# Hybrid encoder step, one core: two buffers of combined inputs, a later subtraction, and other places for the first norm's sums

## What is computed

```python
h = x + 0.5 * swiglu(rmsnorm(x, g_ffn1), w1g, w1u, w1d)       # FFN 1, width 2816
u = rmsnorm(h, g_mix)
h = h + attention(u @ w_in, caches) @ w_out                    # two head groups
h = h + 0.5 * swiglu(rmsnorm(h, g_ffn2), w2g, w2u, w2d)       # FFN 2, the same shape
y = rmsnorm(h, final_norm)
# swiglu(x, wg, wu, wd) = (silu(x @ wg) * (x @ wu)) @ wd
# rmsnorm(x, g)         = x * rsqrt(mean(x * x) + eps) * g
```

## Time and profile before

| | |
|---|---|
| median of 3 runs | 1183.85 us |
| the profiled execution | 1185.94 us |
| its span | 1184.2 us |
| PE busy | 1090.8 us, 92% of the span |
| DVE busy | 709.8 us, 60% |
| ACT busy | 483.7 us, 41% |
| POOL busy | 103.3 us, 9% |
| TensorE clock granted, mean | 0.953 |

### The profile page before, as it was taken

The page is one execution under the profiler, slowest core; times in us unless marked ns, Lnnn a source line. Parts: engine busy times, 40 slices in busy tenths (PEclk is TensorE's granted clock), DMA queues, the critical chain, the costliest instruction groups (busy, mean ns, idle before and its releaser), DMA issues.

```text
span 1184.2 us, 18922 instructions
## 1 busy us (share of the span) xinstructions
PE 1090.8 (92%) x7786; PEld 1054.2 (89%) x7786; DVE 709.8 (60%) x1051; ACT 483.7 (41%) x817; POOL 103.3 (9%) x93
## 2 busy tenths in 40 slices
PE   6969999999999999878998859996999999999995
PEld 5969999999999999766787639996999999999994
DVE  4887852388874333645687644487784248887234
ACT  5435541155553333233334543333663125565221
POOL 5000000000000110412132101200000000000012
PEclk7989999999999999888999869998999999999997
DMA  5222222232223233300111102222223223322202
GB/s 187 71 74 105 78 81 93 89 107 77 102 74 99 70 101 118 118 21 1 46 50 58 50 1 72 89 91 88 72 86 92 91 72 108 107 72 78 95 25 80
DMA packets 22372, 94.42 MB, mean 80 GB/s; under 512 B 2896, under 2 KB 5968, under 8 KB 17552
## 3 DMA queue, kind: packets, MB, share of 16 engines
q1 hardware_dynamic: 22288, 93.23, 23.3%
HBM read 88.24 MB, written 4.98 MB: 79 GB/s over the span
## 4 chain that ended last, share of the span: by engine, by line
PE 75%; DVE 15%; ACT 5%; issue 4%; POOL 2%; DVEq 0%; POOLq 0%; ACTq 0%
PE acc L661 35%; PE acc L592 33%; PE acc L754 3%; DVE w_lo L1284 1%; POOL ssq L1752 1%; ACT c_hi L1025 1%; DVE comb L1389 1%; ACT w_hi L948 1%; PE acc L849 1%; DVE st L1581 1%; DVE st L1574 1%; ACT probs L1167 1%; ACT probs L1177 1%; DVE rrow L1412 1%; DVE probs L1615 1%
## 5 line engine op out<-in xcount | busy, mean ns | idle before, releaser
L1284 DVE TENSOR_TENSOR w_lo<-raw,w_hi 128x1024 fp32r<-128x1024 f32 (+3 forms) x145 | 175.7, 1212 | 269.2 <-ACT w_hi L948 268.9
L661 PE MATMUL acc<-c_hi,w_hi 128*128 128x288 f32 x1008 | 300.3, 298 | 21.3 <-DVE w_lo L1284 21.3
L661 PE MATMUL acc<-c_lo,w_hi 128*128 128x288 f32 x1008 | 301.0, 299 | 0.0
L661 PE MATMUL acc<-c_hi,w_lo 128*128 128x288 f32 x1008 | 300.8, 298 | 0.0
L948 ACT ACTIVATE w_hi<-raw 128x1024 fp32r<-128x1024 f32 (+3 forms) x145 | 148.3, 1023 | 186.6 <-PE acc L592 171.9
L592 PE MATMUL acc<-h_hi,w_hi 128*128 128x288 f32 x960 | 210.7, 300 | 7.8 <-DVE w_lo L1284 7.4
L661 PEld LDWEIGHTS acc<-c_hi,w_hi 128*128 128x128 f32 x1008 | 191.6, 190 | 21.8 <-DVE w_lo L1284 21.8
L592 PE MATMUL acc<-h_lo,w_hi 128*128 128x288 f32 x960 | 209.2, 298 | 0.0
L592 PE MATMUL acc<-h_hi,w_lo 128*128 128x288 f32 x960 | 208.8, 297 | 0.0
L661 PEld LDWEIGHTS acc<-c_lo,w_hi 128*128 128x128 f32 x1008 | 191.5, 190 | 0.0
L661 PEld LDWEIGHTS acc<-c_hi,w_lo 128*128 128x128 f32 x1008 | 191.0, 190 | 0.0
(11 more groups left out here) (198 smaller groups left out, 1369.1 us busy)
## 6 DMA issues: line engine op xcount, KB each, us to landing
raw<-in_w1gu SPq DMA_DIRECT2D x18, 1024.0 KB, 4.8
raw<-in_w2gu SPq DMA_DIRECT2D x18, 1024.0 KB, 4.8
raw<-in_w1d SPq DMA_DIRECT2D x16, 704.0 KB, 4.1
raw<-in_w2d SPq DMA_DIRECT2D x16, 704.0 KB, 4.0
raw<-in_w_qk SPq DMA_DIRECT2D x13, 512.0 KB, 3.8
raw<-in_w1gu SPq DMA_DIRECT2D x8, 512.0 KB, 4.4
raw<-in_w_out SPq DMA_DIRECT2D x8, 512.0 KB, 3.5
raw<-in_w2gu SPq DMA_DIRECT2D x8, 512.0 KB, 3.7
```

The lines of the kernel that those rows point to most:

```text
L661: m = nc.tensor.matmul(acc[:, banks[side(f)], 0:HALF], w_part[:, col:col + P], x_part[:, k, c, :], start=n in (P1, P5, P2) and k == 0 and ...
L1284: return nc.vector.tensor_tensor(cols, src, hi.bitcast(FP32), ALU.subtract).then_inc(split_ready, 1)
```

## The change

- `comb` becomes two buffers, used in turn by columns; `combine` of column j waits for `combine_lo` of column j - 2. The buffers of the snapshots of the seven products (`snap_g`, `snap_u`) are laid over the second one, `w_sum` over the first.
- On DVE `hidden_lo` of a column moves to the next column, ahead of its `gate_out`, and `combine_lo` of a column moves to the next column, behind its `combine`. The last plain column makes both its own `combine_lo` and the one before.
- In FFN 1, column 0, the up block of column 1 is split earlier: ACT's part directly behind `rms`, DVE's directly behind the reciprocal.
- The squares of the first norm are added on DVE, the first sum inside the loop of the inputs' low parts at d = 4, the other six behind that loop. POOL no longer does this, and its loop over the other norms is written out.
- `norm_sums` moves to k-step 6: of the up block in FFN 1, of the gate block in FFN 2.
- The warm-up is 44 matmuls instead of 12.
- `side`, `X_AT` and the slots of `h_hi` and `h_lo` are written in another way with the same values for PLAIN = 4; `if f < KH` is always true here. `o_b` changes its place in memory with `mix_lo`.

```diff
-WARM_UP = 12
+WARM_UP = 44
...
-            comb = sb("comb", [P, 2 * KH, HALF], FP32, ffn_mem)
+            comb = sb("comb", [P, 2, 2 * KH, HALF], FP32, ffn_mem)
...
-            snap_g = sb("snap_g", [P, 2, 2, HALF], FP32, ffn_mem)
-            snap_u = sb("snap_u", [P, 2, HALF], FP32, ffn_mem)
+        snaps = comb[:, 1]
+        snap_g = snaps[:, 0:4, :].rearrange("p (b t) n -> p b t n", b=2)
+        snap_u = snaps[:, 4:6, :]
...
# gate_up_block (TensorE)
-                    if f == 0 and part == 1 and k == 2:
+                    if f == 0 and part == 1 - ffn and k == KD - 2:
                         norm_sums(2 * ffn, NORM_BANK)
...
# plain_gate_up (ACT)
                 if f == 0:
                     rms(NORMS_BEFORE[ffn_no], NORM_BANK)
+                    if ffn_no == 0:
+                        hi_block(("gu", ffn_no, 1, 1))
                 silu(ffn_no, f)
...
-                comb_hi(ffn_no, f)
+                if f < KH:
+                    comb_hi(ffn_no, f)
                 if f + 1 < PLAIN:
-                    hi_block(("gu", ffn_no, f + 1, 1))
+                    if ffn_no or f:
+                        hi_block(("gu", ffn_no, f + 1, 1))
                     hidden_hi(ffn_no, f)
...
# the inputs' low parts (DVE)
                 u_lo_part(0, d)
                 if d == 0 or d == KD - 1:
                     lo_block(("gu", 0, 0, min(d, 1)))
+                if d == KH:
+                    dve.wait_ge(sq_ready, 2)
+                    nc.vector.tensor_tensor(ssq[:], sq[:], up[:], ALU.add).then_inc(ssq_added, 2)
+            for d in range(2, KD):
+
+                dve.wait_ge(sq_ready, d + 1)
+                dve.wait_ge(ssq_added, d)
+                nc.vector.tensor_tensor(ssq[:], ssq[:], (sq, up)[d % 2][:], ALU.add).then_inc(ssq_added, 1)
...
# combine (DVE)
-                if ffn_no or j:
-
-                    dve.wait_ge(c_ready, KH * ffn_no + j)
+                b = comb[:, j % 2]
+                if j > 1 or ffn_no:
+
+                    dve.wait_ge(c_ready, KH * ffn_no + max(j - 1, 0))
...
# plain_gate_up (DVE)
                 if f == 0:
                     dve.wait_ge(rms_done, NORMS_BEFORE[ffn_no] + 1)
                     nc.vector.reciprocal(rrow[:], rrow[:]).then_inc(r_ready, 1)
+                    if ffn_no == 0:
+                        lo_block(("gu", ffn_no, 1, 1))
                     dve.wait_ge(r_ready, NORMS_BEFORE[ffn_no] + 1)
-                gate_out(ffn_no, f)
-                combine(ffn_no, f)
+                else:
+                    hidden_lo(ffn_no, f - 1)
                 if f + 1 < PLAIN:
+                    gate_out(ffn_no, f)
+                    if f < KH:
+                        combine(ffn_no, f)
+                    if f:
+                        combine_lo(ffn_no, f - 1)
                     up_out(ffn_no, f)
-                    lo_block(("gu", ffn_no, f + 1, 1))
+                    if ffn_no or f:
+                        lo_block(("gu", ffn_no, f + 1, 1))
                     hidden(ffn_no, f)
-                    combine_lo(ffn_no, f)
-                    hidden_lo(ffn_no, f)
                 else:
+                    gate_out(ffn_no, f)
+                    combine(ffn_no, f)
+                    combine_lo(ffn_no, f - 1)
                     combine_lo(ffn_no, f)
                     weight_sums(ffn_no, PLAIN)
...
# sums (POOL)
-                with gp.Fori(0, KD - 1 if norm == 3 else KD) as d:
+                for d in range(KD - 1 if norm == 3 else KD):
...
-            clear_sums(0)
-            with gp.Fori(0, KD // 2) as i:
-                for j in range(2):
-
-                    gp.wait_ge(sq_ready, 2 * i + j + 1)
-                    gp.wait_ge(ssq_added, 2 * i + j)
-                    nc.gpsimd.tensor_tensor(ssq[:], ssq[:], (sq, up)[j][:], ALU.add).then_inc(ssq_added, 1)
             sums(1)
```

More of the change, by code:

```diff
@@ L48 @@
 PARTS = 7
+X_AT = PLAIN - 1
+H_SLOTS = max(CHUNK_F, X_AT + KD)
 EPS = 1e-6
@@ L271, in hybrid_step @@
             c_lo = sb("c_lo", [P, KH, PARTS, HALF], FP32R, ffn_mem)
-            h_hi = sb("h_hi", [P, CHUNK_F, TOK], FP32R, ffn_mem)
-            h_lo = sb("h_lo", [P, CHUNK_F, TOK], FP32R, ffn_mem)
-            comb = sb("comb", [P, 2 * KH, HALF], FP32, ffn_mem)
+            h_hi = sb("h_hi", [P, H_SLOTS, TOK], FP32R, ffn_mem)
+            h_lo = sb("h_lo", [P, H_SLOTS, TOK], FP32R, ffn_mem)
+            comb = sb("comb", [P, 2, 2 * KH, HALF], FP32, ffn_mem)
             gate = sb("gate", [P, TOK], FP32, ffn_mem)
             up = sb("up", [P, TOK], FP32, ffn_mem)
-            snap_g = sb("snap_g", [P, 2, 2, HALF], FP32, ffn_mem)
-            snap_u = sb("snap_u", [P, 2, HALF], FP32, ffn_mem)
-        w_sum = comb[:].rearrange("p c n -> p (c n)")[:, 0:4 * PART].rearrange("p (s n) -> p s n", s=4)
-        X_AT = CHUNK_F - KD
+        snaps = comb[:, 1]
+        snap_g = snaps[:, 0:4, :].rearrange("p (b t) n -> p b t n", b=2)
+        snap_u = snaps[:, 4:6, :]
+        w_sum = comb[:, 0].rearrange("p c n -> p (c n)")[:, 0:4 * PART].rearrange("p (s n) -> p s n", s=4)
         with ExitStack() as att_mem:
@@ L297, in hybrid_step @@
             ident = am("ident", [P, P])
+            o_b = am("o_b", [P, 2, TOK_TILES, P])
             mix_lo = am("mix_lo", [P, KD, TOK], FP32R)
-            o_b = am("o_b", [P, 2, TOK_TILES, P])
             sq_o = am("sq_o", [P, TOK_TILES, P])
@@ L407, in side @@
         def side(f):
-            return (f - PLAIN if f < CHUNK_F else f - CHUNK_F) % 2
+            return (f if f < CHUNK_F else f - CHUNK_F) % 2
         def pairs_before(ffn, f):
@@ L1023, in comb_hi @@
                 act.wait_ge(comb_ready, KH * ffn_no + j + 1)
-                nc.scalar.activation(c_hi[:, j, 0, :], comb[:, 0, :], ACT.Copy)
-                nc.scalar.activation(c_hi[:, j, 1:PARTS, :], comb[:, 2:PARTS + 1, :], ACT.Copy).then_inc(chi_ready, 1)
+                b = comb[:, j % 2]
+                nc.scalar.activation(c_hi[:, j, 0, :], b[:, 0, :], ACT.Copy)
+                nc.scalar.activation(c_hi[:, j, 1:PARTS, :], b[:, 2:PARTS + 1, :], ACT.Copy).then_inc(chi_ready, 1)
             def plain_gate_up(ffn_no, f):
@@ L1383, in combine @@
             def combine(ffn_no, j):
-                if ffn_no or j:
-                    dve.wait_ge(c_ready, KH * ffn_no + j)
+                b = comb[:, j % 2]
+                if j > 1 or ffn_no:
+                    dve.wait_ge(c_ready, KH * ffn_no + max(j - 1, 0))
                 for e in range(2):
-                    m = nc.vector.scalar_tensor_tensor(out=comb[:, 2 * e:2 * e + 2, :].rearrange("p c n -> p (c n)"),
+                    m = nc.vector.scalar_tensor_tensor(out=b[:, 2 * e:2 * e + 2, :].rearrange("p c n -> p (c n)"),
                                                        in0=res[:, j + KH * e, :],
@@ L1393, in combine @@
                 then(m)
-                then(nc.vector.tensor_tensor(comb[:, 4:7:2, :], comb[:, 1:4:2, :], comb[:, 0:2, :], ALU.subtract))
-                then(nc.vector.tensor_tensor(comb[:, 5, :], comb[:, 3, :], comb[:, 4, :], ALU.subtract))
-                nc.vector.tensor_tensor(comb[:, 7, :], comb[:, 2, :], comb[:, 5, :], ALU.subtract).then_inc(comb_ready, 1)
+                then(nc.vector.tensor_tensor(b[:, 4:7:2, :], b[:, 1:4:2, :], b[:, 0:2, :], ALU.subtract))
+                then(nc.vector.tensor_tensor(b[:, 5, :], b[:, 3, :], b[:, 4, :], ALU.subtract))
+                nc.vector.tensor_tensor(b[:, 7, :], b[:, 2, :], b[:, 5, :], ALU.subtract).then_inc(comb_ready, 1)
             def combine_lo(ffn_no, j):
+                b = comb[:, j % 2]
                 dve.wait_ge(chi_ready, KH * ffn_no + j + 1)
                 dve.wait_ge(comb_ready, KH * ffn_no + j + 1)
-                nc.vector.tensor_tensor(c_lo[:, j, 0, :], comb[:, 0, :], c_hi[:, j, 0, :].bitcast(FP32), ALU.subtract)
-                nc.vector.tensor_tensor(c_lo[:, j, 1:PARTS, :], comb[:, 2:PARTS + 1, :],
+                nc.vector.tensor_tensor(c_lo[:, j, 0, :], b[:, 0, :], c_hi[:, j, 0, :].bitcast(FP32), ALU.subtract)
+                nc.vector.tensor_tensor(c_lo[:, j, 1:PARTS, :], b[:, 2:PARTS + 1, :],
                                         c_hi[:, j, 1:PARTS, :].bitcast(FP32), ALU.subtract).then_inc(c_ready, 1)
@@ L1732, in clear_sums @@
                 nc.gpsimd.memset(ssq[:], 0.0).then_inc(ssq_zero, 1)
-                gp.wait_ge(ssq_zero, norm + 1)
+                gp.wait_ge(ssq_zero, norm)
             def sums(norm):
```

## The result

| | before | after |
|---|---|---|
| median of 5 runs | 1183.85 us | 1177.92 us |
| lowest to highest | 1183.41 to 1186.06 | 1176.20 to 1178.18 |
| the profiled execution | 1185.94 | 1178.18 |
| its span | 1184.2 | 1176.4 |

The ratio of the runs is 0.9945, 95% interval 0.993 to 0.996: faster by 5.9 us, where 8.9 had been forecast (1175.0, range 1172.3 to 1178.3). The two profiled executions are 7.8 us apart.

What follows compares the result with a forecast made beforehand. PE (busy 92%) was taken as the bound, level with a DVE ring in the plain columns. FFN 1's 8.30 us (3.35 + 4.95) plus FFN 2's 0.55 gave 8.9 us off 1183.85: 1175.0, range 1172.3 to 1178.3.

Steps and rivals of the forecast that it cites:

- The start of FFN 1: FFN 1 up to column 0: sums at 23.69 without the POOL wait, `gate_out` at 30.56 instead of 33.91, 3.35 us earlier.
- the warm-up: Before FFN 1's first block: 32 more matmuls, 7.2 us, start that block near 12.46 instead of 9.03, at full clock.
- The plain columns: FFN 1's four plain columns: `gate_out` distances of 9.48, 12.46 and 10.36 us, together 4.95 us gained.
- The gain of the ring: FFN 1's plain columns: `combine_lo` fills DVE's 2.33 us idle time and periods shorten; part of the 4.95 us.
- FFN 2: Moved sums make PE wait 1.45 us and the reciprocal 1.48 later; periods give back 2.03, net 0.55 us earlier.
- The stretches: At the start, DVE's 128x1024 subtraction takes 2.43 us beside POOL's additions, 1.23 with POOL idle; moving them removes this.
- the other reading: Start of FFN 1: the stretching has another cause and stays, so everything behind the weights' low part comes 1.1 us later.
- The sum: Whole kernel: 8.30 in FFN 1 plus 0.55 in FFN 2, 8.9 us off, 1175.0 against the runs.
- the clock falling in the new waits: Rival 1: clock falls in PE's 2.4 us (FFN 1, column 2) and 1.45 us (FFN 2) waits; 1177, chance 0.14.
- The unshortened ring: Rival 2, plain columns: ACT's copies end last in each period, so only the start counts, 1.9 us; 1182.0, chance 0.05.
- the slow warm-up: Rival 3, start: all 88 warm-up instructions at the low level, first block at 19.8; 1182.3, chance 0.03.
- the slower seven-product columns: Rival 4: ACT and DVE accesses to shared buffers slow each of 36 columns; 1189.4 at 0.4 us each, chance 0.04.

Runs made afterwards that it cites:

- a_again: The changed kernel, unedited, run and profiled a second time; 1177.74 us, ratio 0.9948 to the kernel before.
- a_sums_k0: The changed kernel with FFN 2's norm sums ahead of k-step 0 of the up block; 1170.59 us, ratio 0.9888 to the kernel before.
- a_sums_old2: The changed kernel with FFN 2's norm sums back at k-step 2 of the up block; 1174.22 us, ratio 0.9913 to the kernel before.
- a_pool_adds: The changed kernel with the first norm's additions back on POOL; 1178.97 us, ratio 0.9956 to the kernel before.
- b_again: The kernel before, unedited, run and profiled a second time; 1184.31 us, ratio 1.0009.

## Why the prediction was right, and where its size was off

- **The start of FFN 1.** Predicted: sums 23.69, `gate_out` 30.56. Measured: 24.91 and 31.61, 1.05 late. The term that was mis-sized is the warm-up: its first block was put at 12.46 from a clock that comes up near 4 us, as in the trace of before (its record has the rise at 4.04); in this execution it came at 6.79 and the block started at 13.63. In a_again it came at 4.17 and the block started at 12.38, as forecast. Over the seven profiles with 44 warm-up matmuls the rise lies between 4.07 and 7.02 us and the first block between 12.34 and 13.74, in the same order. The term is not one number, it has a spread of 1.4 us. What lay beside PE was right: the weights' low part ended at 16.7 (16.4), the last addition at 21.66 (21.0).
- **The plain columns.** Distances 9.48, 12.46, 10.36 predicted; 9.36, 12.38, 10.38 measured. From the last `gate_out` to PE 14.00 in both. The gain of the ring stands.
- **FFN 2.** PE's wait 1.45 predicted, 1.35 measured; the reciprocal later by 1.48, measured 1.59; net gain 0.55, measured 0.51. That the moved sums work against the change is shown by a_sums_k0 and a_sums_old2.
- **The stretches.** POOL's additions were taken as the cause; a_pool_adds shows it (2.44 us with them, 1.22 without), and the 1.1 us of the other reading fall away.
- **The sum.** The two places give 7.44 + 0.51 = 7.95 us in the first profiles where 8.85 were summed; the warm-up is the difference. The step to the runs missed by more: the prediction took the profiled execution's 2.09 us above the median as a fixed distance, kept by the change. In the kernel after, the first profile stood 0.26 us above the median. The attention takes 218.2 or 221 us in either kernel, and both first profiles had the long one. A median of five runs shifts with how many of them have it; this is the likely reason why 7.8 us between the profiles became 5.9 between the medians, but only profiled executions show which length they had, so it is not shown. The measured 1177.92 lies inside the range, near an end that was set there for the clock in the waits and for the stretches. Neither of these brought it there, so that part of the hit is luck.
- **Rivals.** The first, the clock falling in the new waits, does not show in the first profile of the kernel after, but it does in a_again, behind FFN 1's 2.12 us wait (granted 0.63 in 48 to 50 us, 0.1 us on the path, the rest hidden by the ring) and behind FFN 2's 1.76 us wait, where it cost 1.1 us. The prediction had placed it in the 1.45 us wait for the sums, and no profile shows it there; it was the one behind it, which the kernel before has as well. The prediction's argument against, that the wait of 1.75 us left the clock up in the trace of before, came from a single execution; the wait left the clock up in 9 of 11 profiles, not in all. The unshortened ring, the slow warm-up and the slower seven-product columns did not occur: the latter have no wait beside the two (9.1 and 8.6 are the 17.7).
- **What stays open.** How often the clock falls behind the 1.75 us wait of FFN 2, and with that how much of the gap between the sum and the medians is FFN 2 and how much the attention. It fell in 2 of the 11 profiles that have this wait (a_again and a_sums_old2); behind FFN 1's 2.12 us wait it fell in 4 of 7. That is too few for a frequency. Why the attention takes one of two lengths also stays open; only its granted clock is known to differ.

## What to carry to other kernels

When two engines close a ring whose length equals the bound's own period, look for its idle time and find work from elsewhere in the ring to put there; it pays at the end of the stage, where the bound engine is out of work and the ring alone decides. A result fetched earlier inside a block delays everything that waits for that block's end: here a 1.35 us wait and 1.2 us of sums inside the gate block cost 2.5 us against the place right behind it. And a warm-up is to end when the operands come, not later: 44 warm-up matmuls give nothing alone, and beside the other steps they cost 2 us against 12 and 3 us against 28 in the traces. That is seen only when the part is taken out of the whole.

## What the runs showed of the hardware

- A pause of PE of 1.75 us is at times followed by a fall of the granted clock to 1.2 GHz (a_again: 0.50 from 769 to 772 us, beginning within 1 us of PE's return; a_sums_old2: 0.50 from 772 to 775) and at times not (the first profile of the kernel after: 1.00), at the same place of the same kernel.
- The warm-up's instructions come at the low pace until the clock record has its first entry, a rise (6.79 us in the first profile of the kernel after, 4.17 in a_again); the view prints 1.00 before it (7 instructions from 6 to 7 us, 11 from 7 to 8).
- POOL and DVE stretch each other: 2.44 us instead of 1.22 for DVE's 128x1024 subtraction, 2.46 instead of 1.43 for POOL's 128x576 addition. Where two began within 0.02 us of each other, the one that began first kept its length (a_pool_adds: DVE 1.23, POOL 2.46; b_again: POOL 1.40, DVE 2.47).
- The same program takes 218.2 or 221 us from the start of the attention to its end, at a mean granted clock of 0.93 to 0.94 or 0.91 to 0.92 in the stretch of 430 to 670 us (13 profiles).
